# Both MLP projections of a streaming encoder trunk as seven block products

## The reference

```
def sqrelu_mlp(h, w_up, w_down):
    return jnp.square(jax.nn.relu(h @ w_up)) @ w_down

for i in range(2):
    x = x + mixer(rms_norm(x, mix_norm_g[i]))
    x = x + sqrelu_mlp(rms_norm(x, mlp_norm_g[i]), mlp_w_up[i], mlp_w_down[i])
```

## Time and profile before

| | |
|---|---|
| time, median of 3 runs | 1467.84 us (1467.72 to 1468.32) |
| span of the profiled execution, first to last instruction | 1466.9 us |
| what lies around that span, against the median | 0.9 us |
| TensorE matmul busy | 1458.1 us (99%) |
| VectorE, GpSimd, ScalarE busy | 825.7, 704.1, 618.7 us (56, 48, 42%) |
| bytes read from memory | 115.91 MB, 81 GB/s over the span |

### The profile page before, as it was taken

The page is one execution under the profiler, slowest core; times in us unless marked ns, Lnnn a source line. Parts: engine busy times, 40 slices in busy tenths (PEclk is TensorE's granted clock), DMA queues, the critical chain, the costliest instruction groups (busy, mean ns, idle before and its releaser), DMA issues.

```text
span 1466.9 us, 29051 instructions
## 1 busy us (share of the span) xinstructions
PE 1458.1 (99%) x10548; PEld 1376.3 (94%) x10548; DVE 825.7 (56%) x1499; ACT 618.7 (42%) x1234; POOL 704.1 (48%) x482
## 2 busy tenths in 40 slices
PE   9999999999999999999999999999999999999999
PEld 7889999999999999999998778787999999999999
DVE  5006716755653635636777676867556537356365
ACT  4423200123534434434637585766135344344352
POOL 8554455443363453553787052452433644535434
PEclk9999999999999999999999999999999999999999
DMA  7222232221143131231343010101221332312312
GB/s 256 85 85 73 76 107 75 68 85 59 44 130 99 60 114 57 86 114 57 115 153 92 30 44 16 43 18 40 78 67 44 123 97 68 114 57 86 115 57 93
DMA packets 36528, 120.32 MB, mean 82 GB/s; under 512 B 6056, under 2 KB 6760, under 8 KB 36208
## 3 DMA queue, kind: packets, MB, share of 16 engines
q1 hardware_dynamic: 32320, 111.83, 24.5%
q10 hardware_dynamic: 4144, 7.65, 1.7%
HBM read 115.91 MB, written 3.55 MB: 81 GB/s over the span
## 4 chain that ended last, share of the span: by engine, by line
PE 48%; DVE 3%; issue 1%; ACT 1%; DVEq 0%
PE ps L749 8%; PE ps L751 8%; PE ps L750 8%; PE ps L910 5%; PE ps L912 5%; PE ps L911 5%; PE ps L1190 2%; PE ps L1007 2%; PE ps L1130 1%; PE ps L1133 1%; PE ps L1012 1%; PE ps L1055 1%; PE ps L1102 1%; DVE lat L1572 1%; PE ps L1141 1%
## 5 line engine op out<-in xcount | busy, mean ns | idle before, releaser
L749 PE MATMUL ps<-h_hi,w_hi 128*128 128x288 f32 x1280 | 380.6, 297 | 0.0
L750 PE MATMUL ps<-h_lo,w_hi 128*128 128x288 f32 x1280 | 377.5, 295 | 0.0
L751 PE MATMUL ps<-h_hi,w_lo 128*128 128x288 f32 x1280 | 376.3, 294 | 0.0
L663 POOL TENSOR_TENSOR w_lo<-raw,w_hi 128x512 fp32r<-128x512 f32 x128 | 171.8, 1352 | 213.8 <-ACT w_hi L1904 213.8
L910 PE MATMUL ps<-op_hi,w_hi 128*128 128x288 f32 x896 | 265.5, 296 | 1.2 <-DVE x L1485 1.2
L911 PE MATMUL ps<-op_lo,w_hi 128*128 128x288 f32 x896 | 264.3, 295 | 0.0
L912 PE MATMUL ps<-op_hi,w_lo 128*128 128x288 f32 x896 | 263.4, 294 | 0.0
L751 PEld LDWEIGHTS ps<-h_hi,w_lo 128*128 128x128 f32 x1280 | 241.1, 188 | 0.0
L749 PEld LDWEIGHTS ps<-h_hi,w_hi 128*128 128x128 f32 x1280 | 239.8, 187 | 1.2
L750 PEld LDWEIGHTS ps<-h_lo,w_hi 128*128 128x128 f32 x1280 | 240.3, 188 | 0.0
L647 POOL TENSOR_TENSOR w_lo<-raw,w_hi 128x1024 fp32r<-128x1024 f32 x60 | 144.2, 2408 | 183.8 <-ACT w_hi L1896 183.8
(11 more groups left out here) (214 smaller groups left out, 2729.3 us busy)
## 6 DMA issues: line engine op xcount, KB each, us to landing
raw<-stream SPq DMA_DIRECT2D x207, 512.0 KB, 3.6
x<-xt SPq DMA_DIRECT2D x8, 288.0 KB, 6.9
out_x<-x ACTq DMA_DIRECT2D x8, 288.0 KB, 2.2
b_bc<-bs ACTq DMA_DIRECT2D x2, 512.0 KB, 6.4
cache_raw<-cache_ct ACTq DMA_DIRECT2D x1, 1024.0 KB, 6.0
v_out<-sgu_grow ACTq DMA_DIRECT2D x1, 512.0 KB, 4.8
ws_sb<-ws ACTq DMA_DIRECT2D x2, 256.0 KB, 4.9
out_v<-v_out ACTq DMA_DIRECT2D x1, 512.0 KB, 4.5
```

Source lines behind the costliest of these rows:

```text
L663: nc.gpsimd.tensor_tensor(block_of(w_lo, b), factor(i, b), block_of(w_hi, b).bitcast(F32), ALU.subtract).then_inc(split_lo, 1)
L749: nc.tensor.matmul(out, l_hi, r_hi, start=first, stop=False)
L750: nc.tensor.matmul(out, l_hi, r_lo, start=False, stop=False)
L751: return nc.tensor.matmul(out, l_lo, r_hi, start=False, stop=last)
```

## The change

`down` keeps its seven products. `up` is now also made of seven products for each of four pairs of hidden tiles, so a quarter has eight pairs (`NPAIRS`) and 56 products in an order that `product_order` writes out. For `up` the streamed operands are the seven blocks and sums of `x` times gain; they are made once for each MLP, in the last eight tiles of the projection ahead of it (`operands_to_mlp`, `project_to_mlp`), whose tiles now come in the order 0, 4, 1, 5, 2, 6, 3, 7.

For `up` the four results of a pair don't grow in banks of their own. Products run in the order A11, S1, S2, A12, S3, S4, A22 (A11 of the next pair right behind A22). ScalarE copies A11's bank into a second one (`copy_first`) and keeps two intermediate sums in SBUF (`keep_sum`); VectorE adds them back (`add_u4`, `add_c22`). Two of the four results are clipped into SBUF (`clip_c11`, `clip_c22`), the others stay in PSUM, are clipped there (`clip_banks`), squared there (`square_banks`), and the differences that `down` wants are formed there (`operand_sum`). TensorE waits for the copies (`copied`), for the sums (`read`) and, at the first pair of `down`, for the last operands (`operand`, `operand_pool`). GpSimd makes the lows of five of the seven weight factors and some of the operands' (`low_hidden`), VectorE those of S1 and S2 and the others'. SyncE loads the two units of pair n+2 when GpSimd's lows of pair n are done.

The sum S1 is formed straight from the two halves of a unit in SBUF, by one VectorE instruction that writes PSUM; ScalarE's lift is gone.

In the first quarter of an MLP, products wait with their last step for the last operands; the norm's sums stand inside A12 and its spread inside S3 of pair 0. Two matmuls (`set_bits`), at the first and the second pair, write a bank that the next product overwrites.

The core of the diff:

```diff
+def product_order():
+
+    order = [(0, A11)]
+    for n in range(PAIRS):
+        order += [(n, f) for f in (S1, S2, A12, S3, S4, A22)]
+        if n + 1 < PAIRS:
+            order.append((n + 1, A11))
+    for n in range(PAIRS, NPAIRS):
+        order += [(n, f) for f in (A11, A12, S1, S2, A22, S4, S3)]
+    return order
...
+            def pairs(mlp, q, unit0, last):
+                for n in range(NPAIRS - 2 if last else NPAIRS):
+                    sp.wait_ge(w_low_set, q * Q_LOW + (mlp * 4 * Q_LOW + lows_of(n)))
+                    for j in (2 * n + 4, 2 * n + 5):
+                        sp.dma_start(raw[:, j % SLOTS, :], stream[q * 16 + (unit0 + j)]).then_inc(raw_loaded[j % SLOTS], 16)
...
+            def quarter(mlp, q, last=False, next_s=None):
+                low_block(mlp, q, 1, A11)
+                for n in range(PAIRS):
+                    if n:
+                        low_hidden(mlp, q, n - 1, 3 * n, slice(5, 7), slice(2, 4))
+                    low_block(mlp, q, n + 1, A12)
+                    low_block(mlp, q, n + 1, S3)
+                    low_block(mlp, q, n + 1, S4)
+                    low_hidden(mlp, q, n, 3 * n + 1, slice(3, 5), slice(0, 2))
+                    low_block(mlp, q, n + 1, A22)
+                    if n + 1 < PAIRS:
+                        low_block(mlp, q, n + 2, A11)
...
+                def set_bits(n):
+
+                    nc.tensor.matmul(ps[:, pair_banks(n)[0], 0:TH], w_hi[:, 0, 0:P], x_operand(B11, 0)[0],
+                                     start=True, stop=True, skip_group_check=True)
...
+                    for n in range(PAIRS):
+                        opening = first and n == 0
+                        weights(q, n, S1)
...
+                        product(n, S1)
+                        weights(q, n, S2)
+                        copied(q, n, 1)
+                        product(n, S2, range(PAIRS - 1) if opening else range(PAIRS))
+                        weights(q, n, A12)
+                        if opening:
+                            product(n, A12, range(PAIRS - 1))
+                            norm_sums(s)
+                            x_lows(3)()
+                            product(n, S2, (PAIRS - 1,))
+                            product(n, A12, (PAIRS - 1,))
+                        else:
+                            product(n, A12)
+                        weights(q, n, S3)
+                        copied(q, n, 2)
+                        if opening:
+                            product(n, S3, range(2))
+                            norm_spread(spread_n)
+                            product(n, S3, range(2, PAIRS))
+                        else:
+                            product(n, S3)
+                        weights(q, n, S4)
+                        read(q, "u4", n)
+                        product(n, S4)
+                        weights(q, n, A22)
+                        copied(q, n, 3)
+                        product(n, A22)
...
+                def first_down(q):
+                    n = PAIRS
+                    weights(q, n, A11)
+                    operand(q, PAIRS - 1)
+                    operand_pool(q, 2 * PAIRS - 3)
+                    product(n, A11, before_last=lambda: operand_pool(q, 2 * PAIRS - 1))
...
+                if part == 0:
+                    dve.wait_ge(raw_loaded[low], q * 64 + loads_of(unit0 + 2 * n))
+                    if n:
+                        dve.wait_ge(low_set, q * Q_DVE_LOW + (mlp * 4 * Q_DVE_LOW + low_count(n - 1, S1)))
+                    nc.vector.tensor_tensor(s1, raw[:, low, 0:512], raw[:, low, 512:UNIT], ALU.add).then_inc(w_sum_set, 1)
...
+                def up(q):
+                    for n in range(PAIRS):
+                        last_sums(mlp, q, n + 1, 0)
+                        if n:
+                            for t in range(4):
+                                operand_sum(q, n - 1, t)
+                        low_sum(mlp, q, n + 1, S1)
+                        last_sums(mlp, q, n + 1, 1)
+                        if n:
+                            low_banks(q, n - 1)
+                        clip_c11(q, n)
+                        add_u4(q, n)
+                        low_sum(mlp, q, n + 1, S2)
+                        first_sums(mlp, q, n + 2, unit0, 0)
+                        add_c22(q, n)
+                        clip_c22(q, n)
+                        first_sums(mlp, q, n + 2, unit0, 1)
+                        clip_banks(q, n)
...
-                def lift(q, i):
-                    slot = 2 * i % SLOTS + 1
-                    act.wait_ge(raw_loaded[slot], q * 64 + loads_of(unit0 + 8 + 2 * i))
-                    if i:
-                        act.wait_ge(low_set, q * Q_DVE_LOW + (dve_l0 + len(DVE_LOW) * (i - 1) + 1))
-                    nc.scalar.copy(ps[:, S1_BANK, :], raw[:, slot, 0:512]).then_inc(lifted, 1)
...
+                def up(q, opening):
+                    for n in range(PAIRS):
+                        B = pair_banks(n - 1)[0]
+                        if n or not opening:
+                            copy_first(q, n)
                         else:
...
+                            norm_root(s)
+                        cast_next(q, n, A11)
+                        cast_next(q, n, S1)
+                        if n:
+                            cast_banks(q, n - 1, 4, slice(0, 3), ps[:, B:B + 3, 0:TH])
+                        keep_sum(q, n, 2)
+                        cast_next(q, n, S2)
+                        cast_next(q, n, A12)
+                        if n:
+                            cast_sums(q, n - 1, 4)
+                        if opening and n == 0:
+                            norm_take(spread_n)
+                        keep_sum(q, n, 3)
+                        cast_next(q, n, S3)
+                        square_hidden(q, n)
+                        cast_next(q, n, S4)
+                        cast_hidden(q, n)
+                        cast_next(q, n, A22)
+                        square_banks(q, n)
```

More of the change, by code:

```diff
@@ L89 @@
-L_GRP, L_O, L_MLP1 = L_IN + 8, L_IN + 24, L_IN + 36
+NPAIRS = 2 * PAIRS
+A11, S1, S2, A12, S4, A22, S3 = range(7)
+FACTORS = 7
+B11, B21, B22, T1, T2, T3, T4 = range(7)
+HIDDEN = {A12: 0, S1: 1, A22: 2, A11: 3, S4: 4, S3: 5, S2: 6}
+OPERAND = {A11: B11, A12: B21, S4: B22, A22: T4, S1: T1, S2: T2, S3: T3}
+ON_POOL, ON_DVE = (A11, A12, S4, A22, S3), (S1, S2)
+def product_order():
[7 more added lines that the diff above has]
+    return order
@@ new lines, with prod_count, made_count, cast_count @@
+PRODUCTS = product_order()
+Q_PROD = len(PRODUCTS)
+Q_LOW, Q_DVE_LOW = len(ON_POOL) * NPAIRS, len(ON_DVE) * NPAIRS
+def prod_count(n, f):
+    return PRODUCTS.index((n, f)) + 1
+def made_count(n, f, among):
+    whole = sum(g in among for _, g in PRODUCTS)
+    before = n - 1 if n else NPAIRS - 1
+    upto = sum(g in among for _, g in PRODUCTS[:prod_count(before, f)])
+    return len(among) + upto - (0 if n else whole)
+def cast_count(n, f):
+    return made_count(n, f, range(FACTORS))
+def low_count(n, f):
+    return made_count(n, f, ON_POOL if f in ON_POOL else ON_DVE)
@@ new lines, in lows_of, with read_count @@
+def lows_of(n):
+    return max(low_count(n, f) for f in ON_POOL)
+DOWN_ADDS = (A11, A12, S1, S2, A22, S4, S3)
+READS = []
+for _n in range(PAIRS):
+    READS += [(what, _n) for what in ("c11", "u4", "c22", "z22", "ab")]
+for _n in range(PAIRS, NPAIRS):
+    READS += [(_f, _n) for _f in DOWN_ADDS]
+Q_READ = len(READS)
+COPIES = [(0, 1)]
+for _n in range(PAIRS):
+    COPIES += [(_n, 2), (_n, 3)] + ([(_n + 1, 1)] if _n + 1 < PAIRS else [])
+Q_COPY = len(COPIES)
+def read_count(what, n):
+    return READS.index((what, n)) + 1
@@ new lines, in quarter @@
+            def quarter(mlp, q, last=False, next_s=None):
[10 more added lines that the diff above has]
+                        low_block(mlp, q, n + 2, A11)
+                for n in range(PAIRS, NPAIRS):
+                    i = n - PAIRS
+                    if next_s is not None and i:
+                        add_square(i - 1, next_s)
+                    if i == 0:
+                        low_hidden(mlp, q, PAIRS - 1, 3 * PAIRS + 1, slice(5, 6), slice(2, 3))
+                    if not last or n + 1 < NPAIRS:
+                        for f in (A11, A12, A22, S4, S3):
+                            low_block(mlp, q, n + 1, f)
@@ L674, in _, with mlp_lows @@
+            def mlp_lows(mlp, next_s):
+                for f in (A11, A12, A22, S4, S3):
+                    low_block(mlp, 0, 0, f)
+                with pool.Fori(0, 3, 1) as q:
+                    quarter(mlp, q)
+                quarter(mlp, 3, True, next_s)
+            mlp_lows(0, 2)
+            for j in range(SLOTS):
+                low_unit(j)
             with pool.Fori(U_IN // SLOTS + 1, U_GRP // SLOTS + 1, 1) as i:
@@ L799, in packed, with token_chunk @@
                                         skip_group_check=True)
```

(2 more changed lines are left out.)

858 lines of the change are left out of this document (518 added, 340 removed).

## The result

The changed kernel takes **1487.01 us** (median of four, 1485.9 to 1488.24) against 1467.78 beside it. The ratio is 1.013, with an interval of 1.0116 to 1.0145: 19 us slower, though 380 matmuls fewer run. The forecast was 1461, with a range up to 1492; the time lies in the range and on the other side of no change.

What follows compares the result with a forecast made beforehand. It took the MLPs to be bound by TensorE's number of matmuls. Fewer matmuls -51.2, `set_bits` +0.5, steady waits +35.2 and openings +8.6 gave -6.9, so 1461 us, with a range of 1432 to 1492.

Steps and rivals of the forecast that it cites:

- rival (4): Behind the 8 largest TensorE waits the clock falls to its lower level for one product: 13 us more, 1474 us; chance 0.06.
- A matmul costs 0.1333, and `up` as products too: In the MLPs each matmul takes 0.1333 us, so 384 fewer in `up` take 51.2 us off.
- Rival (5): In `up`, matmuls made as products don't hold 0.1333 us each; without the gain 1512 us; chance 0.04.
- Steady waits, 35.2: TensorE's waits in the eight MLP quarters, 4.4 us each, the middle of 3.8 and 4.9: 35.2 us added.
- the walk: Queue-by-queue timing of the pairs: 4.9 us lost a quarter with port delays, 3.8 without; 5.3 in each MLP opening.
- The load loop, a turn 0.6 too long: In `up`, one turn from first sum through GpSimd's lows and load takes 11.8 us against a pair's 11.2.
- A rival of hidden loads: Loads land before VectorE wants them; only 2.9 us a quarter and openings of 3 remain: 1446 us; chance 0.21.
- Two inputs from SBUF: The first sum on VectorE may wait out a GpSimd instruction, so a turn can lose up to 1.27 us more.
- The lift's removal, priced at nothing: ScalarE's copy of 512 for each pair goes; ScalarE isn't the bound, so no gain was counted.
- The openings, 8.6: TensorE's waits at each MLP's start: 5.3 us by the walk, a floor of 3, 4.3 taken, 8.6 for both.
- The exit as before: At an MLP's end nothing is lost: x of a low half completes 1.6 us later, but projections use it late.
- the two hidden cases: Loads hidden, 1446 us, chance 0.21, and everything hidden, 1422 us, chance 0.06; midway was given as 1432, the range's lower end.

Runs made afterwards that it cites:

- e1_fill: The changed kernel with 22 matmuls without use in the wait at the first product of `down`, in all 8 quarters: 1475.78 us.
- e3_one_input: The changed kernel with the first sum reading only one half of the unit from SBUF, A21 left out of S1: 1462.85 us.
- e11_before_direct: The kernel before with only the direct sum: S1 formed out of SBUF in one VectorE instruction, no ScalarE copy: 1469.13 us, ratio 1.0007.
- e4_load_swap: The changed kernel with the second unit of a pair, which the first sum wants, requested first: 1460.62 us.
- e6_opening: The changed kernel with A11's bank copy ahead of ScalarE's eighth-tile work and VectorE's last low of `x` ahead of the norm's statistics, in the openings: 1483.05 us.
- e9_lift: The changed kernel with ScalarE's lift back: it copies A21 to PSUM behind S3's cast and VectorE adds A22 there: 1500.89 us.
- e5_gpsimd_order: The changed kernel with hidden 3's low ahead of S4's on GpSimd in pair 3, ScalarE's casts likewise: 1469.93 us.
- e7_all: The changed kernel with load requests swapped, first `down` products' last steps deferred, GpSimd's pair 3 order and the openings' order changed, all together: 1439.32 us.

## Why the prediction was wrong

**What failed: the waits were counted at their own length.** The sum was -51.2 + 0.5 + 35.2 + 8.6, where the last two are TensorE's idle time and nothing else. What such a wait does to the clock stood apart as rival (4), at 8 x 1.6 = 13 us, 1474 and a chance of 0.06, with the reason that no row of before shows a clock under 1.00. But no row of before shows a wait over 1.2 either, so those rows could not speak against it, and the forecast itself put eight waits of 3.5 there. It measured 20.8 us by the mean clock, in twelve stretches: behind each of the eight largest waits, as the rival said, and behind two waits in each opening, which it did not count. A stretch was priced right (1.6 against 1.7); what was wrong is that the term stood in the sum at nothing and that four places were missed. e1_fill shows the cause by itself: with the wait filled by useless matmuls, 11 us came back.

The Trainium skill (TensorE: Matmul & The Clock Gate, section "Why this matters for your kernels") warns of such gaps between bursts of matmuls, and this trace agrees for the eight gaps of 3.4 and more: 1.00 ahead of the gap, 0.50 behind it or from its last half microsecond on. By that page the rival should have been a term of the sum. With its eight stretches -6.9 would have become +6; with the twelve that were measured, +12.

Point by point, in the prediction's own order:

- *A matmul costs 0.1333, and `up` as products too.* Right. The turn of 95.63 us shown above holds 672 matmuls, 89.6 us, waits of 0.61 and 3.40, and a dip of 1.7: 95.3. Rival (5) is out.
- *Steady waits, 35.2.* Right in size, and partly by luck: 28.4 and 7.0 (12.3 less the openings' 5.3), 35.4, where the quarters ran from 4.0 to 5.3 around the 4.4 that was taken. At the first product of `down` the walk said 3.5 and seven of eight were 3.4, put down to GpSimd's low of the hidden, as forecast. The wait of S2 was 0.6 to 0.7 in one to two pairs of each quarter, not 1.0 in one. S4's wait of 0.4 doesn't appear. The late load of one quarter (4.65) made up for part of it.
- *The load loop, a turn 0.6 too long.* Right without the delay of the sum: a turn took 11.78 in e3_one_input, against 11.8, and from request to use the changed kernel took 4.93 at the place shown, against 4.9. With the delay a turn was 12.26. What wasn't seen is how near the loop stood to being harmless. A rival of hidden loads was there (1446), but not that the order of two requests nearly decides it: 1.2 us from request to use, 26 us of the kernel.
- *Two inputs from SBUF.* Right as a mechanism: 1.08 on average over 64 sums, up to 1.8 (the forecast allowed 1.97), beside GpSimd's lows. Its price was too low: the walk had 1.1 a quarter, 9 us, and e3_one_input gives 24 with the clock's share in it, 15.0 of them waits. The copy waits of `up` went with it, which the walk had put at 1.0 a quarter. The delay is carried on from pair to pair, since a turn is 0.48 shorter where the sum is 0.53 shorter. The row that the forecast leaned on was read a little wrong: in the earlier trace rows the instruction of VectorE ended 0.32 after GpSimd's low (362.17 against 361.85), not with it.
- *The lift's removal, priced at nothing.* Right in the old order (e11_before_direct), wrong in the new one, where putting it back costs 14 us: ScalarE isn't the bound by load, but the first sum then waits for it 77.4 us in all, and from the sum the loop goes on.
- *The openings, 8.6.* The walk's 5.3 each was right in sum (5.2 and 5.1, 10.3 in all) and not in its parts: the copy cost 2.7 and 2.6 instead of 1.7, the last low 1.5, the clip 1.1 and 1.0 instead of 1.3, and keep_sum nothing. The value between the walk and the floor was too low by 1.7.
- *The exit as before.* Wrong by 2.6: the stretch from one MLP to the next took 348.3 instead of 345.7. The attention's first projections wait 0.67 and 1.79. VectorE's timeline of the changed kernel there:

```profile
751.84 1.04 DVE L1858 TENSOR_TENSOR cs_q<-cs_sb,gq_row 128x160 f32<-128x160 f32 x1
752.81 2.56 DVE L1861 TENSOR_TENSOR cs_q<-cs_sb,gq_row 128x80 f32<-128x80 f32 x2
755.29 5.41 DVE L1866 TENSOR_TENSOR cT_lo<-cache_raw,cT_hi 128x1024 fp32r<-128x1024 f32 x2
760.62 0.15 DVE L1444 TENSOR_SCALAR var_tok<-ps 128x4 f32<-128x4 f32 x1
```

The kernel before, in which no wait of the attention is over 0.4:

```profile
746.56 0.33 DVE L1543 TENSOR_TENSOR cs_q<-cs_sb,gq_row 128x160 f32<-128x160 f32 x1
746.81 0.38 DVE L1546 TENSOR_TENSOR cs_q<-cs_sb,gq_row 128x80 f32<-128x80 f32 x2
747.11 3.20 DVE L1551 TENSOR_TENSOR cT_lo<-cache_raw,cT_hi 128x1024 fp32r<-128x1024 f32 x2
```

The first three groups read two inputs from SBUF and now meet GpSimd's casts and lows; TensorE waits for `var_tok` behind them. This is read from the traces alone; no experiment changed it.

The account: the openings gave 1.7 more than the sum had, the steady waits 0.2, the exit 2.6 and the clock 20.8. That is 25.3 of the 26.0 between 1461 and 1487.01. With the 1.7 of the clock's part that cost nothing taken off, it is 23.6, and 2.4 stay open.

Some sums of the forecast are off by little and change nothing: GpSimd's load of a pair is 9.2 to 9.6 and not 9.3 to 9.7, the parts named for an opening add up to 5.1 and not 5.3, and midway between the two hidden cases is 1434.

## What to carry to other kernels

Where TensorE is at 99%, a wait that it has never had before is priced twice: at its length, and at the half-speed stretch that may follow (1.7 us here). If the trace of before shows no such wait, it can't show that the clock holds.

When engines work in a loop through a load, compare the turn with the time of a pair first. If they are within about a microsecond, look for the cheapest edit of the order (which of two units is requested first) before costing the rest; it was worth more here than any other change of order.

An engine that isn't the bound can still stand in the chain of every turn. Ask of each instruction which queue it joins, not how busy that engine is.

## What the runs showed of the hardware that was not expected

- The granted clock went to 0.50 at waits of 3.3 us and more every time (25 of 25, in the changed kernel, e4_load_swap, e6_opening and e9_lift), and at shorter ones only sometimes, in otherwise like places: of 2.7 to 2.9, six of eight times in e3_one_input; of 2.3 to 2.4, three of eight times in e5_gpsimd_order and three of seven in e4_load_swap; once of 1.12, in e7_all; and at the 1.79 of the attention in five of the eleven kernels with seven products in `up`. In the openings of the changed kernel the waits of 2.7 and of 1.5 both had a stretch at 0.50; in e1_fill and e4_load_swap the first of these, in the first MLP, had not. What tells the cases apart stays open. The fall came between 0.45 us before the first matmul behind the wait and 0.85 after it, in the eight largest waits of the changed kernel; where it came late, matmuls ran at a spacing of 0.13 until then.
- 22 useless matmuls in each of eight waits made the kernel 11 us faster.
- A VectorE sum of 128x512 with two SBUF inputs waited out GpSimd's instruction. Of the 64 in the changed kernel, 42 started while one ran, and each of them ended 0.56 us after that one ended, for durations of 0.87 to 1.80; the 22 others took 0.69 to 0.70. With a single SBUF input all 64 took 0.68 to 0.70 (e3_one_input), whatever GpSimd did. The Trainium skill (SBUF — State Buffer, section "SBUF: two separate sides") describes that exclusion, and the trace agrees.
